# Forming the T4 sums of the feed-forward weights by accumulating DMA instead of on VectorE

## The chip, the cores and the metric

The kernel runs on one core of a Trainium2 chip. The metric is the device time of one execution in microseconds (us), less being better. Before the change it is 2789.99 us, the median of three runs (2787.24, 2789.99 and 2790.11).

## What is computed

One decoder layer for 512 tokens of width 2048 in float32: RMS norm, sliding-window attention beside RWKV-7 time mixing, gates, an output projection, then a SwiGLU feed-forward part with 5632 hidden channels and a final norm. The change is in the feed-forward part:

```python
h = rms_norm(x, norm_ffn[l])
x = x + (jax.nn.silu(h @ ffn_gate[l]) * (h @ ffn_up[l])) @ ffn_down[l]
return rms_norm(x, norm_final)
```

`ffn_gate` and `ffn_up` are 2048 x 5632, `ffn_down` is 5632 x 2048.

## The kernel before, in words

The front part (attention, time mixing, merge, output projection) takes the first half of the time and is not touched. The feed-forward part is a loop of 17 steps `j`: steps 0 to 10 (`j < CHUNKS`) do 512 gate and 512 up columns each, steps 11 to 16 the down projection. Each step is a two-by-two block product by the Winograd form of Strassen's method, with seven block products in place of eight. The weight is cut into four blocks B11, B12, B22 and B21, each in its own buffer (`wblock11` and so on; `tight` in the two last steps), and three sums replace blocks in place:

- T1 = B12 - B11 in B11's buffer (`t_one`, L1756)
- T3 = B22 - B12 in B12's buffer (`t_three`, L1762)
- T2 = T3 + B11 in B12's buffer, by two accumulating DMAs that GpSimd issues (L774), which add B11 from DRAM onto the buffer
- T4 = T2 - B21 in B21's buffer (`t_four`, L1768)

The products run in the order 1 (B11), 7 (T3), 5 (T1), 6 (T2), 2 (B21), 3 (B22), 4 (T4). A product has `depth(j)` items, 8 in steps 0 to 14 and 6 in steps 15 and 16. An item is one weight tile of 128 x 512. Float32 accuracy comes from splitting each tile: ScalarE copies it to float32r (`ring_high`, the high part, L804), VectorE subtracts that from the tile (`ring_low`, the low part, L1731), and TensorE does six matmuls with them (L2387, L2389, L2391, twice). The ring of high and low parts has four places, so ScalarE can begin an item only when TensorE is done with the item four before it.

Each engine runs its instructions in the order in which they are written; semaphores tie the engines together. VectorE does the low parts and, between them, the sums T1, T3 and T4 and the combinations of the results (`c_lower1`, `hidden2` and others; L1787, L1792, L1821, L1908). Semaphore `sums_ready` counts the sums, and `sum_of` says which count belongs to which. SyncE issues the weight loads (`load_block`, L651) for the next step as soon as a buffer is free, in two halves, in the order 11, 12, 22, 21. GpSimd issues T2's accumulates and, in the down steps, adds the results onto `sum_dram` (`add_sums`, L765). ScalarE's `sums_of_a` in product 4 of a down step first waits for the add of block 22's result to land. In the last step, blocks of that sum come back from DRAM (L716, L720) for the final norm, whose squares ScalarE takes between the high parts.

## Time and profile before

| | |
|---|---|
| median of three runs | 2789.99 us |
| the profiled execution | 2789.86 us |
| its span, first to last instruction | 2788.1 us |
| TensorE (PE) busy | 2734.5 us (98%) |
| VectorE (DVE) busy | 1795.1 us (64%) |
| ScalarE (ACT) busy | 1259.8 us (45%) |
| GpSimd (POOL) busy | 638.1 us (23%) |
| TensorE clock granted, mean | 0.996 of full |

All times in rows are us from the start of the span of that one execution. Busy shares are means over the whole span; what one product of one step does has to be read in its own stretch. An instruction's duration overlaps the next one's start by some 0.08 us on VectorE and ScalarE, so what an instruction adds to a full engine is the distance from start to start. "SPq" is SyncE's queue, where an entry is the issue of a DMA and not its transfer.

### The profile page before, as it was taken

Reading aid. Unit: us, or ns where it says so; the run is one execution under the profiler, and the core shown is the slowest. Engines: PE = TensorE matmul, PEld = TensorE weight load, DVE = VectorE, ACT = ScalarE, POOL = GpSimd, SP = SyncE. Lnnn points to the kernel's source line nnn. Section 1 sums busy time; section 2 is a strip of 40 time slices with the busy share of each in tenths; the row PEclk is TensorE's granted clock in tenths of the full one; section 3 lists DMA queues with packets and bytes.
Section 4 is the critical chain, followed back from the end, with each engine's and each line's share of the span. In section 5 each row is a group of like instructions: output and inputs, shape, how many; then the busy total and the mean of one; then the engine's idle time right before and its main releaser. Section 6 shows DMA issues by size and latency. Waiting matters only on the chain.

```text
span 2788.1 us, 37752 instructions
## 1 busy us (share of the span) xinstructions
PE 2734.5 (98%) x14290; PEld 2205.3 (79%) x14290; DVE 1795.1 (64%) x2893; ACT 1259.8 (45%) x2053; POOL 638.1 (23%) x485
## 2 busy tenths in 40 slices
PE   8999999999999999999999999999999999999997
PEld 7777777777777777888887888888888887888875
DVE  5657365364463564322258878888778888888885
ACT  5444343343343334223335555555555556555555
POOL 2323234233233343544430000000000000111121
PEclk9999999999999999999999999999999999999998
DMA  5222122222222223433445566545654577786873
GB/s 188 76 76 104 65 83 94 76 87 79 77 82 96 73 87 132 158 136 129 139 139 156 166 177 178 153 143 158 177 148 135 152 238 222 188 240 175 216 193 95
DMA packets 190611, 382.51 MB, mean 137 GB/s; under 512 B 9584, under 2 KB 84592, under 8 KB 175728
## 3 DMA queue, kind: packets, MB, share of 16 engines
q1 hardware_dynamic: 146608, 320.55, 33.3%
q0 software_dynamic: 29728, 45.09, 9.9%
q10 hardware_dynamic: 14112, 14.68, 1.5%
q8 instruction: 103, 1.69, 0.2%
q14 instruction: 60, 0.49, 0.1%
HBM read 328.91 MB, written 51.38 MB: 136 GB/s over the span
## 4 chain that ended last, share of the span: by engine, by line
PE 88%; DVE 4%; issue 3%; ACT 2%; DMA 1%; DVEq 1%; POOL 1%; SPq 0%; ACTq 0%; POOLq 0%
PE dense L1994 11%; PE dense L1996 11%; PE dense L1995 11%; PE work L2387 11%; PE work L2389 11%; PE work L2391 11%; PE dense L2387 3%; PE dense L2389 3%; PE dense L2391 3%; PE work L2162 1%; DVEq L1288 1%; PE work L2400 1%; PE work L2214 1%; PE work L1995 1%; PE work L1996 1%
## 5 line engine op out<-in xcount | busy, mean ns | idle before, releaser
L804 ACT ACTIVATE ring_hi<-wblock 128x512 fp32r<-128x512 f32 x840 | 528.6, 631 | 538.9 <-PE work L2391 361.4
L742 POOL TENSOR_TENSOR wlo<-raw,whi 128x512 fp32r<-128x512 f32 x400 | 541.5, 1384 | 896.3 <-ACT whi L804 896.3
L1731 DVE TENSOR_TENSOR ring_lo<-wblock,ring_hi 128x512 fp32r<-128x512 f32 x840 | 573.5, 688 | 175.7 <-ACT ring_hi L804 168.6
L2387 PE MATMUL work<-ring_hi,S_hi 128*128 128x512 f32 x1460 | 573.8, 393 | 15.5 <-DVE ring_lo L1731 15.4
L2391 PE MATMUL work<-ring_lo,S_hi 128*128 128x512 f32 x1460 | 569.5, 390 | 0.0
L2389 PE MATMUL work<-ring_hi,S_lo 128*128 128x512 f32 x1460 | 569.5, 390 | 0.0
L1994 PE MATMUL dense<-H_hi,whi 128*128 128x512 f32 x1208 | 504.9, 418 | 10.1 <-DVE H_lo L1316 8.6
L1996 PE MATMUL dense<-H_hi,wlo 128*128 128x512 f32 x1208 | 473.4, 392 | 0.0
L1995 PE MATMUL dense<-H_lo,whi 128*128 128x512 f32 x1208 | 473.1, 392 | 0.0
L804 ACT ACTIVATE whi<-raw 128x2048 fp32r<-128x2048 f32 (+1 forms) x109 | 198.1, 1820 | 473.0 <-PE dense L1996 388.4
L2387 PEld LDWEIGHTS work<-ring_hi,S_hi 128*128 128x128 f32 x1460 | 275.0, 188 | 81.1 <-DVE ring_lo L1731 21.7
L2391 PEld LDWEIGHTS work<-ring_lo,S_hi 128*128 128x128 f32 x1460 | 274.8, 188 | 57.7
L2389 PEld LDWEIGHTS work<-ring_hi,S_lo 128*128 128x128 f32 x1460 | 275.2, 188 | 55.4
L1994 PEld LDWEIGHTS dense<-H_hi,whi 128*128 128x128 f32 x1208 | 227.7, 188 | 81.7 <-issue 27.0
L1996 PEld LDWEIGHTS dense<-H_hi,wlo 128*128 128x128 f32 x1208 | 227.4, 188 | 50.0
L1995 PEld LDWEIGHTS dense<-H_lo,whi 128*128 128x128 f32 x1208 | 228.0, 189 | 45.0 <-issue 5.8
L774 POOL DMA_DIRECT2D wblock<-w_gu x22 | 28.4, 1290 | 797.9 <-DVE ring_lo L1731 797.9
L2387 PE MATMUL dense<-ring_hi,S_hi 128*128 128x512 f32 x388 | 153.0, 394 | 0.6 <-DVE ring_lo L1731 0.5
L2389 PE MATMUL dense<-ring_hi,S_lo 128*128 128x512 f32 x388 | 151.1, 389 | 0.0
L2391 PE MATMUL dense<-ring_lo,S_hi 128*128 128x512 f32 x388 | 151.0, 389 | 0.0
L1994 PE MATMUL dense<-M_hi,whi 128*128 128x512 f32 x256 | 101.1, 395 | 0.0
L1996 PE MATMUL dense<-M_hi,wlo 128*128 128x512 f32 x256 | 99.8, 390 | 0.0
(336 smaller groups left out, 3391.2 us busy)
## 6 DMA issues: line engine op xcount, KB each, us to landing
raw<-w_slots SPq DMA_DIRECT2D x101, 1024.0 KB, 4.8
wblock<-w_gu SPq DMA_DIRECT2D x88, 1024.0 KB, 9.6
wblock<-w_down SPq DMA_DIRECT2D x60, 512.0 KB, 7.0
wblock<-w_gu POOLq DMA_DIRECT2D x22, 1024.0 KB, 9.8
S_raw<-s_dram SPq DMA_DIRECT2D x14, 1024.0 KB, 8.0
tight<-w_down SPq DMA_DIRECT2D x20, 512.0 KB, 8.2
gates_dram<-gout ACTq DMA_DIRECT2D x32, 256.0 KB, 2.1
gin<-gates_dram SPq DMA_DIRECT2D x16, 512.0 KB, 3.6
```

The source lines that it names most:

```text
L742: done = nc.gpsimd.tensor_tensor(wlo[s][:, at], raw[s][:, at], whi[s][:, at].bitcast(f32), SUB)
L774: pool.dma_start(into, src, accum_op=ADD).then_inc(t2_added[h], 16)
L804: return A.activation(dst, src, ACT.Copy, scale=scale)
L1288: V.drain()
L1731: V.tensor_tensor(ring_lo[w % RING][:], of_tile(j, source[product], k), ring_hi[w % RING][:].bitcast(f32), SUB).then_inc(ring_lo_ready, 1)
L1994: PE.matmul(bank[:], whi[s][:, wk], hi[:, k, :], start=(k == first), stop=False)
L1995: PE.matmul(bank[:], whi[s][:, wk], lo[:, k, :], start=False, stop=False)
L1996: done = PE.matmul(bank[:], wlo[s][:, wk], hi[:, k, :], start=False, stop=(k == last))
L2162: done = PE.matmul(g_bank(2 * t + e)[:, half:half + 2 * P], src[heads[e], tok], zq[heads[e], t].rearrange("p a n -> p (a n)"), start=True, ...
L2387: PE.matmul(banks[a][:], S_hi[product][:, k, tok], high[:], start=(k == 0 and product not in (3, 2)), stop=False, skip_group_check=True)
L2389: PE.matmul(banks[a][:], S_lo[product][:, k, tok], high[:], start=False, stop=False, skip_group_check=True)
L2391: done = PE.matmul(banks[a][:], S_hi[product][:, k, tok], rest[:], start=False, stop=(k == depth(j) - 1), skip_group_check=True)
```

## The change

T4 is no longer computed on VectorE. ScalarE negates B21 in place, tile by tile, after product 2 has read it: tiles 0 to 3 among the last high parts of product 2, the rest among the first of product 3 (`negate`). When half the block is negated, and T2 stands, GpSimd issues a DMA from B12's buffer to B21's with an add, both in SBUF (`t4_added`). Product 4's high parts wait for that. B12's buffer is read later than before, so SyncE loads the next B12 after B22, and behind a wait for both accumulates. And VectorE's T1 sums, which need that block, begin at the third item of product 1 and are made up from item `n - 3` on. The other edits reuse semaphores. The core of the diff:

```diff
-SUM0 = [sum(3 * depth(i) for i in range(j)) for j in range(STEPS)]
+SUM0 = [sum(2 * depth(i) for i in range(j)) for j in range(STEPS)]
...
+        def half_of(j, h):
+
+            return slice(h * HK // 2 * P, min((h + 1) * HK // 2, depth(j)) * P)
...
-                sp.wait_ge(sums_ready, sum_of(j, 4, depth(j) - 1))
-                load_block(j + 1, 12)
                 sp.wait_ge(ring_lo_ready, after(j, 3))
                 load_block(j + 1, 22)
+                for h in range(2):
+                    sp.wait_ge(t4_added[h], 16 * (j + 1))
+                load_block(j + 1, 12)
                 load_s(j, 3)
                 sp.wait_ge(ring_lo_ready, after(j, 4))
                 load_block(j + 1, 21)
...
                         pool.dma_start(into, src, accum_op=ADD).then_inc(t2_added[h], 16)
+                for h in range(2):
+                    pool.wait_ge(t2_added[h], 16 * block_dmas(j, 11, h))
+                    pool.wait_ge(negated, SUM0[j] // 2 + min((h + 1) * HK // 2, depth(j)))
+                    pool.dma_start(blocks(j)[21][:, :, half_of(j, h)], blocks(j)[12][:, :, half_of(j, h)],
+                                   accum_op=ADD).then_inc(t4_added[h], 16)
...
+                elif product == 4:
+                    act.wait_ge(t4_added[2 * k // HK], 16 * (j + 1))
...
+            def negate(j, k):
+
+                act.wait_ge(ring_lo_ready, item_of(j, 2, k) + 1)
+                tile = blocks(j)[21][:, :, k * P:(k + 1) * P]
+                copy(tile, tile, -1.0).then_inc(negated, 1)
...
                     ring_high(j, 2, k)
+                    if k >= 4:
+                        negate(j, k - 4)
...
                     ring_high(j, 3, k)
+                    if k < 4:
+                        negate(j, depth(j) - 4 + k)
...
                         ring_low(j, 1, k)
-                    t_one(j, k)
-                    if k >= n - 2:
+                    if 2 <= k < n - 3:
+                        t_one(j, k - 2)
+                    if k == n - 3:
+                        t_one(j, n - 5)
+                        t_one(j, n - 4)
+                    if k == n - 2:
+                        t_one(j, n - 3)
+                        t_one(j, n - 2)
                         fence()
-                        t_three(j, k - n + 2)
+                        t_three(j, 0)
+                    if k == n - 1:
+                        t_one(j, n - 1)
+                        fence()
+                        t_three(j, 1)
...
-                    if k in (1, 2):
-                        fence()
-                        t_four(j, k - 1)
...
-                    if k + 2 < n:
-                        fence()
-                        t_four(j, k + 2)
```

VectorE in product 1 of a gate/up step, before. A row is one instruction in program order with the tile that it writes and those that it reads; `ring_lo` rows are low parts, `wblock11<-wblock12` is T1, `u3buf` is `c_lower1`.

```order
L1731 TENSOR_TENSOR ring_lo0_196<-wblock11_188,ring_hi0_192 128x512
L1756 TENSOR_TENSOR wblock11_188<-wblock12_189,wblock11_188 128x4x128
L1731 TENSOR_TENSOR ring_lo1_197<-wblock11_188,ring_hi1_193 128x512
L1756 TENSOR_TENSOR wblock11_188<-wblock12_189,wblock11_188 128x4x128
L1731 TENSOR_TENSOR ring_lo2_198<-wblock11_188,ring_hi2_194 128x512
L1756 TENSOR_TENSOR wblock11_188<-wblock12_189,wblock11_188 128x4x128
L1731 TENSOR_TENSOR ring_lo3_199<-wblock11_188,ring_hi3_195 128x512
L1756 TENSOR_TENSOR wblock11_188<-wblock12_189,wblock11_188 128x4x128
L1787 TENSOR_TENSOR u3buf_201<-u3buf_201,work4 128x512
```

The same place after the change, from the first low part of product 1 to T3's first sum (`wblock12<-wblock22`).

```order
L1754 TENSOR_TENSOR ring_lo0_196<-wblock11_188,ring_hi0_192 128x512
L1754 TENSOR_TENSOR ring_lo1_197<-wblock11_188,ring_hi1_193 128x512
L1754 TENSOR_TENSOR ring_lo2_198<-wblock11_188,ring_hi2_194 128x512
L1779 TENSOR_TENSOR wblock11_188<-wblock12_189,wblock11_188 128x4x128
L1754 TENSOR_TENSOR ring_lo3_199<-wblock11_188,ring_hi3_195 128x512
L1779 TENSOR_TENSOR wblock11_188<-wblock12_189,wblock11_188 128x4x128
L1804 TENSOR_TENSOR u3buf_201<-u3buf_201,work4 128x512
L1754 TENSOR_TENSOR ring_lo0_196<-wblock11_188,ring_hi0_192 128x512
L1779 TENSOR_TENSOR wblock11_188<-wblock12_189,wblock11_188 128x4x128
L1804 TENSOR_TENSOR u3buf_201<-u3buf_201,work5 128x512
L1754 TENSOR_TENSOR ring_lo1_197<-wblock11_188,ring_hi1_193 128x512
L1779 TENSOR_TENSOR wblock11_188<-wblock12_189,wblock11_188 128x4x128 x2
```

The first two low parts have no T1 behind them any more; two of the later ones have two.

SyncE's queue, the loads for the next step in a gate/up step, before:

```order
L651 DMA wblock11_188<-w_gu 128x4x512 [waits ring_lo_ready]
L651 DMA wblock11_188<-w_gu 128x4x512
L651 DMA wblock12_189<-w_gu 128x4x512 [waits sums_ready]
L651 DMA wblock12_189<-w_gu 128x4x512
L651 DMA wblock22_190<-w_gu 128x4x512 [waits ring_lo_ready]
L651 DMA wblock22_190<-w_gu 128x4x512
L651 DMA wblock21_191<-w_gu 128x4x512 [waits ring_lo_ready]
L651 DMA wblock21_191<-w_gu 128x4x512
```

and after:

```order
L656 DMA wblock11_188<-w_gu 128x4x512 [waits ring_lo_ready]
L656 DMA wblock11_188<-w_gu 128x4x512
L656 DMA wblock22_190<-w_gu 128x4x512 [waits ring_lo_ready]
L656 DMA wblock22_190<-w_gu 128x4x512
L656 DMA wblock12_189<-w_gu 128x4x512 [waits t4_added1,t4_added0]
L656 DMA wblock12_189<-w_gu 128x4x512
L656 DMA wblock21_191<-w_gu 128x4x512 [waits ring_lo_ready]
L656 DMA wblock21_191<-w_gu 128x4x512
```

B12's load has gone behind B22's and waits for the accumulates; B21's load is queued behind it.

GpSimd's queue in the first down step after the change; before, the two rows of L784 were not there, and the first `sum_dram` row followed T2's directly.

```order
L780 DMA wblock12_189<-w_down 128x4x256 [waits ring_lo_ready]
L780 DMA wblock12_189<-w_down 128x4x256
L784 DMA wblock21_191<-wblock12_189 128x4x512 [waits negated,t2_added0]
L784 DMA wblock21_191<-wblock12_189 128x4x512 [waits negated,t2_added1]
L771 DMA sum_dram<-c22buf_202 128x2x512 [waits c_ready,xt_stored]
```

The add of block 22's result onto `sum_dram` is now issued behind both accumulates of T4.

## Rows read from the trace of the kernel before

**Rows 1.** Busy time by stretch: a gate/up step's length, a down step's

```profile
1759.20:1835.70 76.50, 76.48 (x346) 63.18 (x345) 62.16 (x97) 39.19 (x65) 2.56 (x2) 1.00 0.57 162
2447.70:2524.20 76.50, 75.86 (x335) 62.28 (x334) 67.41 (x95) 44.58 (x65) 10.04 (x8) 1.00 0.81 220
```

**Rows 2.** What TensorE waited for, 1455 to 2740: total, times, longest

```profile
PE work L2387 <- DVE ring_lo L1731: 15.4, 10, 6.2
```

**Rows 3.** Chain of waits, the last loads of final sums: start, length

```profile
2709.95 13.79 DMA fin<-sum_dram
```

**Rows 4.** Timeline of VectorE, step 4, products 1 and 7

```profile
1780.58 0.69 DVE L1731 TENSOR_TENSOR ring_lo<-wblock,ring_hi 128x512 fp32r<-128x512 f32 x1 [0.17 <-ACT ring_hi L804]
...
1783.17 0.68 DVE L1756 TENSOR_TENSOR wblock<-wblock,wblock 128x512 f32<-128x512 f32 x1
1783.78 0.69 DVE L1731 TENSOR_TENSOR ring_lo<-wblock,ring_hi 128x512 fp32r<-128x512 f32 x1
...
1792.70 0.69 DVE L1731 TENSOR_TENSOR ring_lo<-wblock,ring_hi 128x512 fp32r<-128x512 f32 x1
```

**Rows 5.** Timeline of TensorE, step 4: product 7's first and fourth item

```profile
1789.18 0.39 PE L2387 MATMUL dense<-ring_hi,S_hi 128*128 128x512 f32 x1
...
1793.44 0.50 PE L2387 MATMUL dense<-ring_hi,S_hi 128*128 128x512 f32 x1
```

**Rows 6.** Timeline of ScalarE, step 4: product 2's last item, products 3 and 4

```profile
1828.72 0.63 ACT L804 ACTIVATE ring_hi<-wblock 128x512 fp32r<-128x512 f32 x1 [0.73 <-PE work L2391]
...
1834.70 0.64 ACT L1116 ACTIVATE work<-work,rstd 128x512 f32<-128x512 f32 x1
...
1840.96 0.63 ACT L804 ACTIVATE ring_hi<-wblock 128x512 fp32r<-128x512 f32 x1 [0.73 <-PE work L2391]
...
1846.40 0.63 ACT L804 ACTIVATE ring_hi<-wblock 128x512 fp32r<-128x512 f32 x1 [0.73 <-PE work L2391]
```

**Rows 7.** Timeline of VectorE, step 12, product 7's first low part

```profile
2417.38 0.68 DVE L1731 TENSOR_TENSOR ring_lo<-wblock,ring_hi 128x512 fp32r<-128x512 f32 x1
```

**Rows 8.** Timeline of TensorE, step 12, product 7's first item

```profile
2418.21 0.47 PE L2387 MATMUL dense<-ring_hi,S_hi 128*128 128x512 f32 x1
```

**Rows 9.** Timeline of VectorE, step 11, product 1's second low part

```profile
2326.14 0.68 DVE L1731 TENSOR_TENSOR ring_lo<-wblock,ring_hi 128x512 fp32r<-128x512 f32 x1
```

**Rows 10.** Timeline of GpSimd, step 4: T2's two accumulates

```profile
1793.68 1.28 POOL L774 DMA_DIRECT2D wblock<-w_gu  x1 [72.58 <-DVE ring_lo L1731]
1798.08 1.28 POOL L774 DMA_DIRECT2D wblock<-w_gu  x1 [3.12 <-DVE ring_lo L1731]
```

**Rows 11.** Line L774 in 1780 to 1800, those two: issue to landing

```profile
DMA to landing us min/median/max: 9.5/9.8/10.1
```

**Rows 12.** DMA queues in 1793 to 1809: packets, MB, share of 16 engines

```profile
q0 software_dynamic: 1056, 2.10, 77.0%
```

**Rows 13.** DMA queues in 1760 to 1786, plain loads: the same columns

```profile
q1 hardware_dynamic: 3440, 6.82, 79.2%
```

**Rows 14.** Timeline of SyncE, the six loads of B12, B22, B21

```profile
1761.95 12.78 SPq L651 DMA_DIRECT2D wblock<-w_gu  x6
```

**Rows 15.** Line L651 in 1763.1 to 1763.5, the third of the six: landing

```profile
DMA to landing us min/median/max: 10.7/10.7/10.7
```

**Rows 16.** Timeline of VectorE, step 5, product 1's third T1 sum

```profile
1855.84 0.68 DVE L1756 TENSOR_TENSOR wblock<-wblock,wblock 128x512 f32<-128x512 f32 x1
```

**Rows 17.** Timeline of ScalarE, step 15: second of product 3, product 4's first, `sums_of_a`

```profile
2677.17 0.63 ACT L804 ACTIVATE ring_hi<-tight 128x512 fp32r<-128x512 f32 x1 [0.73 <-PE dense L2391]
...
2684.99 0.63 ACT L804 ACTIVATE ring_hi<-tight 128x512 fp32r<-128x512 f32 x1 [0.75 <-PE work L2391]
...
2689.65 0.58 ACT L804 ACTIVATE c22buf<-dense 128x512 f32<-128x512 f32 x1
```

**Rows 18.** Timeline of GpSimd, step 15: block 22's sum

```profile
2680.07 1.20 POOL L765 DMA_DIRECT2D sum_dram<-c22buf  x1 [25.53 <-DVE c22buf L1908]
```

**Rows 19.** What TensorE waited for, 1459.5 to 1468.6, in step 0

```profile
PE work L2387 <- DVE ring_lo L1731: 4.5, 1, 4.5
```

More of the change, by code:

```diff
@@ L145, in sum_of @@
     n = depth(j)
-    first = {5: k + 1 + max(k - n + 2, 0), 7: (n + 2 * k if k < 2 else n + 1 + k), 4: 2 * n + 1 + k}[product]
+    first = {5: k + 1 + max(k - n + 2, 0), 7: (n + 2 * k if k < 2 else n + 1 + k)}[product]
     return SUM0[j] + first
@@ L440, in build_layer @@
         sums_ready, t2_added = sem("sums_ready"), [sem(f"t2_added{h}") for h in range(2)]
+        negated, t4_added = sem("negated"), [sem(f"t4_added{h}") for h in range(2)]
         ring_hi_ready, ring_lo_ready, item_done = (
@@ L449, in build_layer @@
         added = {b: sem(f"added{b}") for b in block_at}
-        fin1_loaded, fin0_loaded, gin_before = sem("fin1_loaded"), gin_loaded, 8 * KD
+        fin1_loaded, fin0_loaded, gin_before, xin_before = xin_loaded[0], gin_loaded, 8 * KD, 8 * KD
         fin_ready, fin_squared, fin_turned, resid_copied = (
@@ L454, in build_layer @@
         tail_inverse, tail_spread, scale_copied = sem("tail_inverse"), sem("tail_spread"), sem("scale_copied")
-        pool_out, out_ready, out_stored = sem("pool_out"), sem("out_ready"), sem("out_stored")
+        pool_out, out_ready, out_stored = sem("pool_out"), sem("out_ready"), xin_loaded[1]
         heads = [slice(e * HD, e * HD + HD) for e in range(2)]
@@ L730, in _ @@
                                  ).then_inc(out_stored, 16)
-            sp.wait_ge(out_stored, 2 * 16 * len(OUT_PARTS))
+            sp.wait_ge(out_stored, xin_before + 2 * 16 * len(OUT_PARTS))
         @block.gpsimd
@@ L1763, in t_three @@
                                 ).then_inc(sums_ready, 1)
-            def t_four(j, k):
-                block_wait(dve, j, 21, k)
-                V.tensor_tensor(of_tile(j, 21, k), of_tile(j, 12, k), of_tile(j, 21, k), SUB
-                                ).then_inc(sums_ready, 1)
             def s_late_low(place_of, product):
@@ L1863, in _ @@
                         dve.wait_ge(item_done, after(j, 7))
-                        dve.wait_ge(fin1_loaded, 64)
+                        dve.wait_ge(fin1_loaded, xin_before + 64)
                         add_to(fin1[21][a], bank_of(j, 7)[a][:])
```

## The prediction, made before the changed kernel ran

> **What bounds the kernel now.** I read busy time by stretch first. In a gate/up step TensorE is busy 76.48 us of 76.50, in a down step 75.86 [rows 1]. VectorE, from which the change takes work, is busy 62 to 67 us there: it has spare time, but TensorE has none to give back. Next, what TensorE waited for: between 1455 and 2740 it stood 15.4 us behind low parts, ten times, 6.2 us of it once in the last step [rows 2]. That is all that a faster VectorE could win, and the 6.2 us belong to the final sums coming back by DMA [rows 3]. So the question is not what the change frees, but whether it moves something into TensorE's way. For that I read the timelines of one steady step.
>
> VectorE is not evenly loaded. Step 4's fifth low part of product 1 still waits for its high part (0.17 us idle, at 1780.58); from there to the low part at 1792.70, the fourth item of product 7, no idle is marked [rows 4]. That low part ends at 1792.70 + 0.69 = 1793.39, and TensorE starts on it at 1793.44 [rows 5]: 0.05 us apart. Product 7's first item to its fourth took 4.26 us, where three items at TensorE's pace are 4.08 (1.36 us each: four high parts of product 4 from 1840.96 to 1846.40 [rows 6]). So VectorE has just used up its whole lead there. Products 1 and 7 are the one place in a step where VectorE is on the path, and T4 is not computed there.
>
> **T4 off VectorE.** Its 132 sums go (8 in a deep step), each 0.60 us from start to start by the like sum T1, 1783.17 to 1783.78 [rows 4]. They stood in products 2 and 3, which in steady steps hold TensorE up nowhere. Gain: 0 there. Where VectorE is behind in products 2 and 3 (step 15, by its S splits) I give some tenths, inside the term for that step.
>
> **T1 later.** This is the costly part. Before, each low part of product 1 had a T1 behind it, in time in which VectorE would have waited for ScalarE anyway. Now the first two have none, and these two sums come after the fifth item, in the stretch without idle. Up to the fifth low part nothing changes in time, since ScalarE sets it. From there to product 7's fourth item VectorE has the same work as before and two T1 sums more: 2 x 0.60 = 1.20 us. T3 comes late by the same, and so do product 7's high parts, which wait for it, but each is still ready before its low part. With 0.05 us of margin, TensorE stands the 1.20 us, in two to four pieces over product 7.
>
> Steps 1 to 10 repeat this pattern: 10 x 1.20 = 12.0 us. In step 12 the tightest item is product 7's first: low part done at 2417.38 + 0.68 = 2418.06, TensorE at 2418.21, 0.15 apart [rows 7, 8], so 0.10 more is left than the 0.05: 1.10 us, and steps 12 to 15 alike: 4.4 us. Step 11 starts with VectorE in arrears: its second low part, at 2326.14, comes without idle before it [rows 9], and the two sums that are missing there first let it catch up. Between 0 and 1.20 I take 0.4. In step 0 the first low parts are made ahead of the loop; the two sums leave an early wait of TensorE shorter and make a later one longer, 0. In step 16 the 1.10 us come ahead of the wait for the final sums, which ends by DMA and not by TensorE's time: 0 (at most 1.1).
>
> **The accumulate.** The trace has no transfer within SBUF that adds, but T2's add from DRAM with the same shape: 9.5 and 10.1 us from issue to landing, issued 4.4 us apart [rows 10, 11], the two taking 77% of 16 us, or 12.3 us of all engines, for 2.10 MB [rows 12]. The first half of T4 is negated after product 2's last high part: 1828.72 + 0.54 + 0.63 = 1829.9, issued some 0.3 us later (as long as T2's issue at 1793.68 comes after the low part's end at 1793.39), landing at 1830.2 + 9.5 = 1839.7. Product 4's first high part starts at 1840.96 [rows 6]: 1.3 us to spare. A high part's successor on ScalarE starts 0.54 us after it, as L1116 at 1834.70 does (its high part is five paces before 1840.96, at 1834.16). The second half's last negation takes that place and ends at 1835.3; issued at 1835.6, landed at 1845.7, wanted at 1846.40: 0.7 us to spare, and behind that stands the ring's lead. So 0 in deep steps. That lead is at most 2.7 us: a high part starts when TensorE ends the item four before, so three items (4.08 us) ahead, less some 1.4 us for the high and the low part. So 0 in deep steps. Bounds: plain loads take 79.2% of 26 us for 6.82 MB, 3.0 us a MB [rows 13] against 5.9 for the adds; at that pace T4 lands up to 6 us sooner and still gains 0. At half T2's pace the pair needs 24.6 us and lands some 12 us later, about 9 us beyond the lead in each of the 17 steps. I take T2's own pace, the nearest row.
>
> The Trainium skill ("DMA: Bandwidth & Descriptors", section on the anatomy of one DMA on the SWDGE path) gives 2.0 us plus bytes over 436 GB/s for a DMA from GpSimd, an estimate of 4.4 us for 1 MB. The trace disagrees for adds: 9.5 us [rows 11]. By the page the allowances for T4 below would be 0 and the sum some 3 us less.
>
> **The negations.** 132 on ScalarE, about 0.54 us more each beside a high part in a pace of 1.36 us: 0.54 + 0.54 = 1.08, it fits. Where L1116 stands too, 1.62 once or twice, inside the lead. 0.
>
> **Loads.** B22 goes out when product 3's low parts are done, about 1841.1 (one pace before 1840.96, plus a high and a low part), B12 at T4's landing, 1845.7. Before, the third load of a row lands at 1763.16 + 10.7 = 1773.9, 11.9 us after the first was issued at 1761.95 [rows 14, 15]. So B12's first half lands at 1841.1 + 11.9 = 1853.0, and with up to 1.3 us lost to T4's tail at 1854.4. The first T1 now stands where the third stood, 1855.84 [rows 16]: 1.4 us to spare. Then 0, but thin: VectorE would wait in front of all low parts, and every us late is a us of each step. In down steps SyncE's nine to eleven issues and the three result adds run at the same time (DMA share 0.81 [rows 1]), and there it is a matter of nothing to 2 us a step.
>
> The Trainium skill (same page, "Issuing engines are not separate DMA queues") says that transfers of all issuers share the 16 engines. If T4's adds therefore slow B22's and B12's loads by more than the 1.3 us allowed, it is the first rival below.
>
> **Shallow step 15.** Here product 3 has six items, and T4's first half is ready only after its second high part: 2677.17 + 1.2 = 2678.4, issued 2678.7, landed 2688.2, wanted at 2684.99 [rows 17]. ScalarE is 3.2 us late, TensorE behind its lead some 0.7. Then block 22's add, issued at 2680.07 before [rows 18], goes out behind T4's second half, near 2683, and through the same queue: it lands near 2694.5, where `sums_of_a` (2689.65 [rows 17]) wants it, 5 us late, some 2 of it beyond the lead. This also moves the chain of final sums that ends the wait in step 16. I take 3.0 us together, bounds 0 and 7.
>
> **Sum.** 12.0 + 0.4 + 4.4 + 3.0 = 19.8 us. 2789.86 + 19.8 = 2809.7; the profiled execution is 0.13 us under the median shown. Forecast: 2810 us, slower by 0.7%. Its own range is 2803 to 2818 (step 11 and 15 at their ends, step 16's 1.1, a us of loads in some down steps).
>
> **Rivals.**
>
> 1. The transfers are late, beside the late sums. Place: B12's first half lands after the first T1's place. It decides from 1.4 us more than reckoned, and each further us costs 16. At 2 us late per step: 2810 + 32 = 2842. For it: the engines are full in both rows that matter, and B22's and B12's loads had them to themselves before. Against: T4 is nearly through when B22's data starts. With T4 itself at half pace it would be 2940 and more.
>
> 2. The same time, 2790. The two late sums are absorbed, since the arrears of VectorE are made up in a way that I do not see, or the stall shortens a later one. Against: 0.05 us between low part and matmul [rows 4, 5], and no later stall in steady steps to shorten [rows 1].
>
> 3. Faster: VectorE without T4 carries a longer lead into the other stalls [rows 2] in steps 10 to 15, and takes them away. Place: product 4 and the next product 1; it decides if the lead at the start of product 1 is VectorE's and not the ring's. Price: of 15.4 us, 6.2 are the final sums' and 4.5 lie in step 0 [rows 19], so about 4.7 us: 2785. Against: the ring has four places, and the high part waits for TensorE, not VectorE, on nearly every item of product 4 [rows 6].
>
> **Chances.** Forecast 0.63, rival 1 0.22, rival 2 0.09, rival 3 0.06. A measurement of this kernel can tell about 0.2%, 5.6 us, from no change. So slower by more 0.85, within 0.09, faster 0.06. The range: 2797 to 2845, which leaves out rivals 2 and 3 and the far end of rival 1.
>
> **What would show it.** Steps 1 to 10 last 1.2 us longer each, with TensorE waiting for low parts in items one to four of product 7 and not in products 2, 3 and 4. No low part of product 4 follows a ScalarE wait for DMA, except in step 15. The accumulate lands in 9 to 10.5 us. VectorE's busy time falls by about 132 x 0.69 = 91 us, ScalarE's rises by some 80. Wrong if TensorE's waits stand in product 1 (B12 late) or 4 (T4 late), or if a steady step keeps its length.

## The result: 46 us slower, and the profile after

The changed kernel takes 2836.3 us (median of 4 runs, 2835.87 to 2836.71) against 2789.98 (4 runs, 2787.24 to 2790.11), measured beside it: a ratio of 1.017, 95% interval 1.0157 to 1.0183. The forecast was 2810, so the sign was right and the loss was more than twice what I reckoned. Its profiled execution spans 2834.3 us, 46.2 more than before's.

The head of the page of the changed kernel, two lines of its queues and two of its DMA issues (KB each, median us from issue to landing):

```profile
PE 2750.9 (97%) x14290; PEld 2206.6 (78%) x14290; DVE 1715.6 (61%) x2761; ACT 1324.9 (47%) x2185; POOL 681.6 (24%) x519
...
q1 hardware_dynamic: 146608, 320.55, 32.2%
q0 software_dynamic: 47680, 79.70, 16.8%
...
wblock<-wblock POOLq DMA_DIRECT2D x30, 1024.0 KB, 8.4
...
wblock<-w_gu POOLq DMA_DIRECT2D x22, 1024.0 KB, 9.9
```

VectorE is busy 79.5 us less than before, ScalarE 65.1 us more (forecast: about 91 less and 80 more), and T4's accumulates land in 8.4 us in the median, a little sooner than T2's 9.9. None of these three explains 46 us. Where the time went is read from the length of each step, from its first matmul to the next step's first (step 16: to within 0.1 us of the next matmul behind it), in the timeline of TensorE. This table has them, in us, for all kernels of the study; "late sums" and the other names are the experiments of the next section.

| kernel | steps 1 to 9, mean | 10 | 11 | 12 | 13 | 14 | 15 | 16 |
|---|---|---|---|---|---|---|---|---|
| before | 78.26 | 79.59 | 79.94 | 77.24 | 76.32 | 76.31 | 59.85 | 73.50 |
| changed | 79.52 | 83.25 | 80.45 | 85.76 | 84.13 | 84.14 | 70.13 | 72.63 |
| late sums alone | 79.48 | 80.83 | 80.42 | 78.45 | 77.50 | 77.53 | 60.89 | 74.23 |
| gate/up alone | 79.50 | 83.37 | 79.98 | 77.26 | 76.32 | 76.35 | 59.89 | 73.33 |
| B12 first | 79.50 | 83.52 | 80.40 | 79.05 | 78.17 | 77.74 | 63.96 | 81.12 |
| sum 22 first | 79.51 | 83.25 | 80.39 | 90.06 | 77.49 | 82.91 | 63.61 | 75.17 |
| old T1 order | 78.91 | 84.55 | 79.21 | 88.01 | 84.89 | 84.98 | 71.21 | 75.64 |
| late loads, no T4 transfer | 79.46 | 80.79 | 80.36 | 78.41 | 77.49 | 77.57 | 60.51 | 71.63 |
| B12 and sum 22 first | 79.51 | 83.47 | 80.39 | 82.44 | 77.66 | 79.49 | 62.31 | 80.52 |
| B12 first, S later | 79.50 | 80.79 | 80.37 | 78.46 | 78.01 | 77.52 | 62.31 | 78.81 |
| repaired, old T1 order | 78.26 | 79.88 | 79.95 | 77.25 | 81.75 | 76.68 | 62.60 | 78.49 |
| and shallow steps as before | 78.26 | 79.59 | 79.97 | 77.25 | 82.53 | 76.67 | 61.05 | 72.57 |
| and S later in step 10 only | 78.26 | 79.55 | 79.98 | 77.92 | 79.05 | 76.99 | 64.12 | 72.50 |

Steps 1 to 9 are 1.26 us longer each, as forecast. Step 10 is 3.7 longer, and steps 12 to 15 are 34.4 us longer together (8.5, 7.8, 7.8, 10.3), where the forecast had 7.4 (4.4 for the late sums and 3.0 for the shallow step). Step 16 is even 0.9 shorter. Steps 1 to 16 together lose 49 us; the span loses 46.2, since step 0 is 0.9 us shorter and starts 1.9 sooner. Its start lies between 1455.6 and 1458.6 us in the thirteen kernels, which all have the same front part, so a us or two of a difference between two spans can come from there.

What TensorE waited for in the changed kernel, 2345 to the end (total, times, longest), the answer to [rows 2]; in before the same stretch has 10.3 us behind low parts:

```profile
PE work L2408 <- DVE ring_lo L1754: 21.9, 16, 3.6
PE dense L2408 <- DVE ring_lo L1754: 10.6, 7, 4.1
```

The low parts are late because VectorE is held in front of them. What it waited for in that stretch (these waits for loads exist only in the changed kernel):

```profile
DVE wblock L1779 <- DMA wblock<-w_down: 18.3, 3, 6.7
DVE tight L1779 <- DMA tight<-w_down: 10.3, 2, 5.5
```

Line 1779 is T1, which reads B12. So in each of steps 12 to 16 the first T1 waits for that load, 28.6 us in all. Here it is in step 12, first the timeline of VectorE, then that of TensorE, which uses the low part of 2427.09:

```profile
2419.57 0.69 DVE L1754 TENSOR_TENSOR ring_lo<-wblock,ring_hi 128x512 fp32r<-128x512 f32 x1 [0.67 <-ACT ring_hi L815]
2426.48 0.69 DVE L1779 TENSOR_TENSOR wblock<-wblock,wblock 128x512 f32<-128x512 f32 x1 [6.22 <-DMA wblock<-w_down]
2427.09 0.68 DVE L1754 TENSOR_TENSOR ring_lo<-wblock,ring_hi 128x512 fp32r<-128x512 f32 x1
```

```profile
2427.83 0.50 PE L2408 MATMUL work<-ring_hi,S_hi 128*128 128x512 f32 x1 [3.58 <-DVE ring_lo L1754]
```

Of 6.22 us, 2.6 are TensorE's lead and 3.6 are lost. VectorE, with no lead left, then costs 0.83 at product 1's last item, where the late sums alone cost 0.36. Why is the load late? GpSimd's timeline around it, then what the queues did in the same 16 us (packets, MB, share of 16 engines):

```profile
2394.78 1.29 POOL L784 DMA_DIRECT2D wblock<-wblock  x1 [31.52 <-ACT wblock L815]
2400.22 1.29 POOL L784 DMA_DIRECT2D wblock<-wblock  x1 [4.14 <-ACT wblock L815]
2400.97 1.76 POOL L771 DMA_DIRECT2D sum_dram<-c22buf  x1
```

```profile
q0 software_dynamic: 1328, 2.62, 98.7%
q1 hardware_dynamic: 297, 0.30, 5.6%
```

T4's two halves and block 22's result sum fill the 16 DMA engines from 2396 to 2412. SyncE has issued B22 from 2405.33 on, but nearly none of its data has moved by 2412. Its issues slow down with it: the pieces of B22 take up to 2.1 us each to issue, so B12's, free to go since T4 landed at 2400.22 + 8.72 = 2408.94, go out from 2412.30 to 2416.33. The first two, which T1 waits for, are issued at 2412.3 and 2413.6:

```profile
L656 SPq DMA_DIRECT2D wblock<-w_down x2: 1216/1621/2026, 2412.3 to 2413.6; - x2
...
  DVE wblock L1779: 6.2, 1
...
DMA to landing us min/median/max: 12.0/12.5/12.9
```

2413.56 + 12.89 = 2426.45, and T1 starts at 2426.48.

The same two stretches as [rows 1] of a gate/up and a down step (start:end, length, PE, PEld, DVE, ACT and POOL busy, clock, DMA share, GB/s), and a piece of the second at half clock:

```profile
1759.50:1836.00 76.50, 75.89 (x341) 61.95 (x340) 57.51 (x89) 42.02 (x70) 4.72 (x4) 1.00 0.66 182
2506.00:2590.10 84.10, 78.68 (x337) 63.92 (x336) 61.47 (x87) 47.75 (x72) 12.62 (x10) 0.98 0.81 203
...
2429.00:2432.40 3.40, 3.40 (x9) 2.21 (x8) 3.31 (x7) 0.63 (x1) 0.79 (x1) 0.50 1.12 369
```

The third line is a price on top. From 1.1 us after the wait that ends at 2427.83 the granted clock is 0.50 for 3.4 us (1.2 GHz in place of 2.4), and a matmul takes 0.43 us from start to start (2430.83 to 2431.26) in place of 0.23. From step 10 to 16 the changed kernel has five such stretches, 20.5 us, at five of its six waits of 2.7 us or more (three of them begin while TensorE still waits, so a part of them costs nothing), where before has one of 6.8 us: 13.7 us more at half speed, up to 6.8 us of the 46.

### The profile page after: what moved, and what is told of

Read it like the earlier page. It is cut to its first block, busy times and chain, and to the rows that moved or that the text cites. A ratio compares the mean times of both kernels' runs of the same rounds, so it can differ in the third digit from the quotient of the medians.

```text
span 2834.3 us, 37704 instructions
## 1 busy us (share of the span) xinstructions
PE 2750.9 (97%) x14290; PEld 2206.6 (78%) x14290; DVE 1715.6 (61%) x2761; ACT 1324.9 (47%) x2185; POOL 681.6 (24%) x519
## 3 DMA queue, kind: packets, MB, share of 16 engines
q0 software_dynamic: 47680, 79.70, 16.8%
## 4 chain that ended last, share of the span: by engine, by line
PE 79%; DVE 9%; DMA 5%; ACT 3%; issue 2%; DVEq 2%; SPq 1%; POOL 0%; ACTq 0%; POOLq 0%
PE dense L2015 11%; PE dense L2017 11%; PE dense L2016 11%; PE work L2408 9%; PE work L2410 9%; PE work L2412 9%; DVE ring_lo L1754 2%; PE dense L2408 2%; PE dense L2412 2%; PE dense L2410 2%; DVE wblock L1779 2%; DVEq L1311 2%; DVE wblock L1785 2%; DMA wblock<-w_down 1%; DMA wblock<-wblock 1%
## 5 line engine op out<-in xcount | busy, mean ns | idle before, releaser
L2015 PE MATMUL dense<-H_hi,whi 128*128 128x512 f32 x1208 | 504.7, 418 | 10.1 <-DVE H_lo L1339 8.6
L2408 PE MATMUL dense<-ring_hi,S_hi 128*128 128x512 f32 x388 | 156.2, 403 | 14.2 <-DVE ring_lo L1754 13.9
L784 POOL DMA_DIRECT2D wblock<-wblock x30 | 38.6, 1286 | 524.3 <-ACT wblock L815 524.3
L2408 PEld LDWEIGHTS dense<-ring_hi,S_hi 128*128 128x128 f32 x388 | 73.6, 190 | 39.7 <-DVE ring_lo L1754 23.1
```

The lines of the kernel that those rows point to most:

```text
L2015: PE.matmul(bank[:], whi[s][:, wk], hi[:, k, :], start=(k == first), stop=False)
L2408: PE.matmul(banks[a][:], S_hi[product][:, k, tok], high[:], start=(k == 0 and product not in (3, 2)), stop=False, skip_group_check=True)
```

## The experiments

The intervals are 95%. The kernel before was run again beside each group of experiments, and it differs by up to 2 us between groups, so a difference of that size between two medians of different groups says little; before measured 2787.92 us (7 runs, 2785.57 to 2790.16) beside the first four, 2787.81 (7 runs, 2786.83 to 2791.19) beside the next four, and 2789.07 and 2789.42 (10 runs each) beside the last three.

**Late sums alone.** The kernel before with T1's new order and nothing else.

```diff
-                    t_one(j, k)
+                    if 2 <= k < n - 3:
+                        t_one(j, k - 2)
...
```

> The kernel before with one part of the change: T1's sums stand where the change puts them (first one behind the third low part of product 1, two each behind the sixth and seventh). T4 stays on VectorE, the loads keep their order. If the late sums are a cause by themselves, as forecast (1.2 us in steps 1 to 10, some 1.1 in 12 to 15, 0.4 in 11, less up to 1 in step 0): 2805 us, 2802 to 2808, with waits for low parts in product 7 only. If the 1.2 us that the changed kernel shows in its steps 1 to 9 come from T4's transfers or the negations instead: 2790.

Measured 2804.89 us (4 runs, 2802.87 to 2806.78), ratio 1.0061 (1.0044 to 1.0078). As expected. By steps: 12.3 us in steps 1 to 10 (forecast 12.0), 0.5 in step 11 (0.4), 4.65 in steps 12 to 15 (4.4).

**Gate/up alone.** T4 by DMA, B12's later load and the late sums in steps 0 to 10 only; the down steps as before.

```diff
-                for h in range(2):
+                for h in range(2 if j < CHUNKS else 0):
                     pool.wait_ge(t2_added[h], 16 * block_dmas(j, 11, h))
...
```

> The changed kernel with the change in the eleven gate/up steps only; steps 11 to 16 have T4 on VectorE, T1 behind every low part and the old order of loads, except the loads for step 11, which step 10 issues in the new order. If the excess over the forecast lies in the down steps: 2790 + 11.5 for steps 1 to 10, less 0.9 in step 0, and 0 to 3 for step 10's waits in product 4: 2800 to 2804. If the transfers of the gate/up steps carried part of the loss into the down steps: 2810 or more.

Measured 2802.08 (2800.3 to 2802.45), ratio 1.0049 (1.0033 to 1.0066). As expected: the excess belongs to the down steps, but for step 10, which keeps its 83.37.

**B12 first.** The changed kernel with the loads of B12 and B22 in the old order, B12's still behind T4's landing.

```diff
+                for h in range(2):
+                    sp.wait_ge(t4_added[h], 16 * (j + 1))
+                load_block(j + 1, 12)
                 sp.wait_ge(ring_lo_ready, after(j, 3))
                 load_block(j + 1, 22)
-                for h in range(2):
-                    sp.wait_ge(t4_added[h], 16 * (j + 1))
-                load_block(j + 1, 12)
```

> The changed kernel with B12's load ahead of B22's in SyncE's queue, still behind both waits for T4's accumulates. Theory Q (queueing): in the down steps B12 is late because its pieces are issued and moved behind the five pieces of B22; then they land some 6 to 8 us earlier, before the first T1 sum wants them, TensorE's waits in product 1 of steps 12 to 16 and the half clock after them go, and the time is 2808 to 2814. Theory T (traffic): B12 is late because T4's accumulates land late and take the engines; then the order matters little: 2825 to 2833. Gate/up steps keep their 79.5 us under both.

Measured 2817.67 (2816.96 to 2819.86), ratio 1.0107 (1.009 to 1.0123). It lies between the two expectations, over the 2814 of the queueing theory and well under the 2825 of the traffic theory. It wins 18.6 us back, 16.6 if each kernel is taken against its own before, and steps 12 to 15, 324.2 us in the changed kernel, take 298.9, 4.5 over the late sums alone. So T4's landing itself comes early enough for B12; what is lost is lost between it and B12's data. Step 10 stays at 83.5: its one wait of 1.85 us brings 3.4 us at half clock with it, so it isn't the length of a wait alone that decides. Step 16 grows to 81.1: part of what is won comes back there as waits of 5.6 us at most, with 6.8 and twice 3.4 us at half clock.

**Sum 22 first.** The changed kernel with block 22's result sum issued between T4's halves, since ScalarE waited 11.3 us in all for it (its line is below).

```diff
+                    if h == 0 and CHUNKS <= j < LAST:
...
+                        add_sums(j, 22, c22buf)
```

> The changed kernel with the add of block 22's result onto DRAM issued between T4's two accumulates instead of behind both (down steps only). ScalarE's waits for that add, 11.3 us in three pieces (steps 12, 14 and 15), should go nearly. If they are worth their share of TensorE's waits in product 4 (1.8, 1.1 and 3.3 us, with the half clock in step 15): 2828 to 2832. If T4's second half, now some 3 us later, delays product 4 and B12's load by as much: no change or slower, 2836 to 2845.

Measured 2829.34 (2828.02 to 2830.82), ratio 1.0148 (1.0131 to 1.0165): 7.0 us better than the change (4.9 against each one's own before), within the first of the two expectations. ScalarE's wait for the sum is down to 0.7 us, and steps 13 and 15 fall by 6.6 and 6.5. But steps 12 and 14 are 90.1 and 82.9 us: the file of transfers (all that is queued for the 16 engines, in order) has another order and the same length, so T4's second half is late in product 4 instead (TensorE waits 2.5 and 1.5 us there in step 12), and in steps 12, 14 and 16 B12 still is in product 1.

**Late loads, no T4 transfer.** Late sums alone, and from the loads for step 12 on B22's load first and B12's behind product 4's fourth low part. Now place and traffic are apart.

```diff
-                sp.wait_ge(sums_ready, sum_of(j, 4, depth(j) - 1))
-                load_block(j + 1, 12)
+                if j < CHUNKS:
+                    sp.wait_ge(sums_ready, sum_of(j, 4, depth(j) - 1))
+                    load_block(j + 1, 12)
                 sp.wait_ge(ring_lo_ready, after(j, 3))
                 load_block(j + 1, 22)
+                if j >= CHUNKS:
+                    sp.wait_ge(ring_lo_ready, item_of(j, 4, 3))
+                    load_block(j + 1, 12)
```

> The kernel before with T1's late order (as in the experiment on the late sums alone, 2804.9 us) and one more edit: from step 11 on, block 22's load goes first and block 12's goes out behind it and behind product 4's fourth low part, which is the moment at which the changed kernel issues it. T4 stays on VectorE, so no T4 transfer shares the queues. Theory 'place' (block 12's late place behind block 22's five pieces is enough): VectorE again waits some 4.5 to 6 us for block 12 at product 1's third low part in steps 12 to 16, TensorE 2 to 3.6 us and some tenths after it, so each of these steps is 4 to 6.5 us longer than in the experiment on the late sums: 2825 to 2838. Theory 'traffic' (T4's two transfers, and block 22's result sum that queues behind them, are what push block 12 out): block 12 lands some 3 us and more sooner, and the time is 2805 to 2813. Values between say that both have a share, and the share is (time - 2805) / (2836 - 2805).

Measured 2804.18 (2802.1 to 2804.9), ratio 1.0054 (1.0037 to 1.0071): the late sums' time, share 0 for the place. The queues of this kernel in 2396 to 2412, then the load of B12's second piece, issued at 2409.5 behind all of B22:

```profile
q1 hardware_dynamic: 2449, 1.92, 37.8%
q0 software_dynamic: 272, 0.52, 23.1%
```

```profile
L651 SPq DMA_DIRECT2D wblock<-w_down x1: 739/739/739, 2409.5 to 2409.5; - x1
...
DMA to landing us min/median/max: 7.4/7.4/7.4
```

It lands at 2416.9, 9.6 us sooner than in the changed kernel, and T1 wants it at 2419.81. The difference between the two q0 lines is T4: 98.7% - 23.1% of 16 us, 12.1 us of all engines. B12 behind B22 is harmless with the engines free, and behind T4 and the sum it costs 6 to 6.7 us a step (steps 12 to 15 of the changed kernel against B12 first); B12 first behind T4 costs 0.2 to 0.7 in the deep ones. It takes both together: a place behind B22, and T4's transfers in front. (This kernel also has no negations on ScalarE and T4's sums on VectorE; the rows above show the load itself on time.)

**Old T1 order.** The changed kernel with T1's sums back at their places.

```diff
-                    if 2 <= k < n - 3:
-                        t_one(j, k - 2)
...
+                    t_one(j, k)
```

> The changed kernel with one thing undone: T1's sums stand where they did before, the first behind product 1's first low part. The loads and T4's transfers stay as changed. Theory 'coupled' (the late order was needed because block 12 now lands late): in a gate/up step block 12's first half lands at 1856.9 and the first T1 would be wanted near 1853.1, so VectorE waits some 3.8 us in front of the low parts, of which about 2 us are idle time that it has in product 1's first items anyway; TensorE loses 1.5 to 2.5 us a step in place of the 1.2 of the late order, and in the five down steps the wait for block 12 grows by up to two items (2.7 us) less the 1.1 of the late sums: 2836 + 10 x (0.3 to 1.3) + 5 x 1.6 = 2847 to 2857. Theory 'needless' (the late order only costs, and block 12 is early enough in gate/up steps): steps 1 to 10 get their 1.2 us back and the whole lands at 2822 to 2830.

Measured 2839.98 (2837.46 to 2842.09), ratio 1.0182 (1.0165 to 1.0199). Neither expectation. Steps 1 to 9 take 78.91, 0.6 us less than with the late order, though B12 lands as late: there the late order costs more than the wait that it avoids. In the down steps TensorE now waits at product 1's second item:

```profile
2425.17 0.79 PE L2398 MATMUL work<-ring_hi,S_hi 128*128 128x512 f32 x1 [6.41 <-DVE ring_lo L1754]
```

The five waits are 5.4 to 6.4 us, where the late order had 2.7 to 4.1. With the half clock that comes with them (10.2 us from 2421, which begins inside the first wait, and 6.8 in each of the four others) these steps take 404.7 us against 396.8. The late order is worth something there, 7.9 us in five steps, and by the experiment on the repaired kernel below only because the load is late.

**B12 and sum 22 first.** Both repairs.

> The changed kernel with both repairs tried singly so far: block 12's load ahead of block 22's (alone 2817.7 us) and the result sum of block 22 between T4's two halves (alone 2829.3, 7 us better than the change). If the two gains belong to different waits (block 12 for VectorE's T1; the result sum for ScalarE's reuse of its buffer in steps 12, 14 and 15), they add up: 2817.7 less 2 to 5 = 2812 to 2816. If they are the same wait seen twice (the whole file of transfers moved up), the second adds nothing, or T4's second half, now behind the result sum, costs in product 4: 2816 to 2822.

Measured 2823.2 (2822.2 to 2824.1), ratio 1.0123 (1.0106 to 1.014): 5.5 us worse than B12 first alone, just outside the second expectation, on its side. Steps 12 and 14 take 82.4 and 79.5; TensorE waits 0.92 and 1.92 us in product 4 of step 12 for T4's second half, now behind the sum. The gains don't add.

**B12 first, S later.** B12 first, and the load of product 2's S rows moved behind both block loads. It goes out in steps 10, 12 and 14 only, beside T4's transfers.

```diff
-                load_s(j, 2)
...
                 load_block(j + 1, 22)
+                load_s(j, 2)
                 load_s(j, 3)
```

> The changed kernel with block 12's load first (alone 2817.7 us) and the load of product 2's S rows (steps 10, 12 and 14 only) moved from product 2's end, beside T4's transfers, behind both block loads. In step 10 of the changed kernel this S load is issued at 2313.68, and T4's second half, issued at 2315.46, lands 13.9 us later where 8.6 is usual; TensorE then waits 0.84 + 1.92 us in product 4. If the S load is what holds the transfer up, step 10 falls from 83.5 to 80.7 - 81.3 us, steps 12 and 14 by some tenths to 1 us, and the whole to 2812.5 to 2815.5. If T4's second half is late by its own wait and not by the S load, step 10 stays at 83 to 84 us and the whole at 2817 to 2820.

Measured 2812.85 (2811.72 to 2816.17), ratio 1.0091 (1.0074 to 1.0108). As expected: step 10 falls from 83.5 to 80.8, the value of the late sums alone. The transfer that made it long (the same happens in steps 12 and 14, 12.4 and 12.5 us to landing in the changed kernel, 8.7 and 8.8 here), T4's second half at 2315.5 in the changed kernel, and the same one here:

```profile
L784 POOL DMA_DIRECT2D wblock<-wblock x1: 1287/1287/1287, 2315.5 to 2315.5; - x1
...
DMA to landing us min/median/max: 13.9/13.9/13.9
```

```profile
L784 POOL DMA_DIRECT2D wblock<-wblock x1: 1284/1284/1284, 2315.0 to 2315.0; - x1
...
DMA to landing us min/median/max: 9.7/9.7/9.7
```

Steps 1 to 14 are those of the late sums within 0.5 us. What is left lies in steps 15 and 16, 1.4 and 4.6 us of the 6.3 by which the two profiled spans differ.

**Repaired, old T1 order.** B12 first, S later, and T1 at its old places.

> The changed kernel with block 12's load first, the S load behind both block loads (these two alone: 2812.9 us), and T1's sums back in their old order. Theory 'load order was the only reason for the late order': with block 12 first, its first half lands at 1852.6 in a gate/up step and at 2413.2 in a down step, where the old order wants the first T1 near 1855.3 and 2414.6: 2.7 and 1.3 us to spare. Then the late sums' cost goes (12.3 us in steps 1 to 10, 0.5 in step 11, about 3.5 in steps 12 to 14 and up to 1 in step 15), steps 1 to 9 fall to 78.25 - 78.35, and the time is 2794 to 2799. Theory 'margin too thin': VectorE, at T1's old place, waits for block 12 in the down steps, or for block 22 at T3, which now also comes 1.2 us sooner; then steps 12 to 14 stay at 78 us and more, and the time is 2800 to 2808.

Measured 2803.82 (5 runs, 2802.61 to 2808.18), ratio 1.0057 (1.0043 to 1.0071). Neither expectation as a whole. The time is in the second's range, the reason is not the second's: neither B12 nor B22 is late in steps 12 to 14. The cost of the late sums is gone: steps 1 to 12 are before's within 0.3 us, so with B12 first nothing asks for the late order there. But step 13 takes 81.75, with a wait of TensorE of 3.5 us in product 5.

**And shallow steps as before.** T4 of steps 15 and 16 on VectorE again; 120 of the 132 sums stay with the DMA (the expectation miscounts them as 118).

> The same kernel with one more edit: in steps 15 and 16, with six items a product, T4 is computed on VectorE as in the kernel before; T4 by DMA stays in steps 0 to 14. Theory 'shallow steps hold the rest': step 15 falls back to 59.9 and step 16 to 73 - 74 us, so the time is that of the kernel before within what can be told, 2787 to 2793, with 118 of 132 sums off VectorE and nothing won by it. Rival: T4 by DMA costs elsewhere too, or the freed VectorE wins something once nothing is late: then the time is over 2794, or under 2785.

Measured 2797.83 (6 runs, 2795.39 to 2802.64), ratio 1.0035 (1.0023 to 1.0047): over the first expectation, so its rival is right that T4 costs elsewhere too. Steps 15 and 16 lose 1.6 and 5.9 us of what they had; step 13 stays at 82.5. ScalarE's timeline there:

```profile
2511.73 1.91 ACT L818 ACTIVATE S_hi<-S_raw 128x2048 fp32r<-128x2048 f32 x1 [5.98 <-DMA S_raw<-s_dram]
```

**And S later in step 10 only.**

```diff
+                if j != CHUNKS - 1:
+                    load_s(j, 2)
...
+                if j == CHUNKS - 1:
+                    load_s(j, 2)
```

> The repaired kernel with T4 by DMA in steps 0 to 14 (2797.8 us), with the load of product 2's S rows moved behind the block loads in step 10 only; in steps 12 and 14 it goes out at product 2's end again. In that kernel ScalarE waits 8.4 us in all, up to 6.0, for S rows, and step 13 takes 82.5 us where 76.3 is usual, with TensorE's wait of 4.5 us in product 5: the S load of step 12, now late, should be the reason. If it is, step 13 falls to 76.3 - 76.7, steps 12 and 14 gain at most 0.6 us, and the time is 2789 to 2793, that of the kernel before within what can be told. If the wait in step 13 has another source (block 11's load, the result sums), step 13 stays over 80 us and the time at 2795 to 2800.

Measured 2796.18 (6 runs, 2794.5 to 2800.45), ratio 1.0027 (1.0015 to 1.0039). A miss of the first expectation; the time is in the second's range, but step 13 isn't over 80. It falls by 3.5 us to 79.05, so the late S load was part of it, but step 12 gains 0.7 and step 15 3.1 again. The 0.7 is T4 once more: with the S load beside it its second half lands after 11.9 us in place of 8.6, and TensorE waits 1.31 us in product 4 of step 12 in place of 0.64. With T4 in the queues the down steps 12 to 16 take 370.1 us with the one order and 370.6 with the other, 363.2 before. I can move the 7 us from step to step, not away; which transfer costs the rest of them stays open. In steps 1 to 11 of these two kernels, where before has 0.54 to 0.73 of the engines busy, T4 by DMA is free, and VectorE's spared time has won nothing there, 78.26 us a step as before. None of the kernels beats the one before.

## Why the prediction was right in sign and wrong in size

**T4 off VectorE, 0: held.** 79.5 us less work, and no step shorter for it.

**T1 later, 12.0 + 0.4 + 4.4: held.** In step 4 of the changed kernel TensorE waits at product 7's first item and at its fourth, and nowhere else in the step.

```profile
1790.94 0.50 PE L2408 MATMUL dense<-ring_hi,S_hi 128*128 128x512 f32 x1 [0.35 <-DVE ring_lo L1754]
...
1795.88 0.50 PE L2408 MATMUL dense<-ring_hi,S_hi 128*128 128x512 f32 x1 [0.21 <-DVE ring_lo L1754]
```

The marked waits do not sum to 1.2; the rest lies in slower starts around them (1793.57 to 1794.02 in the same product). The experiment on the late sums measured 17.0 us for them as a whole, against 16.8.

**The accumulate, 0 in deep steps: held, except in steps 10, 12 and 14.** In step 4 it lands in 7.8 and 8.1 us, sooner than T2's 9.5 and 10.1 [rows 11], and no high part of product 4 waits. Its engine time is T2's: 12.2 us for 2.10 MB against 12.3 [rows 12]. In steps 10, 12 and 14 an S load (1 MB, in step 14 0.75) is issued 1.8 to 2.1 us before T4's second half, which I had not looked for. The half then lands after 13.9, 12.4 and 12.5 us, and product 4 waits for it, against my sign that this happens in step 15 alone: 2.4 us of step 10, and 1.2 and 1.1 us more than before of TensorE's waits in product 4 of steps 12 and 14, shared with the sum of block 22 behind it.

**Loads: this is the step that failed.** I wrote "there it is a matter of nothing to 2 us a step" and took 0. For gate/up steps I worked out the landing of B12's first half (1854.4; the trace has 1846.51 + 10.43 = 1856.9, 2.5 us later and still without a loss, since the first T1 comes at about 1858). For the down steps I did not do the sum. It was in the rows: [rows 1] has the engines busy 0.81 of 76.5 us, 62 us, and T4 adds 12.3 [rows 12], 0.97, an estimate. I charged T4's 12 us of engine time to T4's own landing and only 1.3 us of it to the loads behind it. Block 22's sum, which I made late for step 15, stands in the same file in every down step: 3.7 us (23.1% of 16) between T4 and B22. Measured from the table: 324.2 us in steps 12 to 15 against 294.4 with the late sums alone, 29.8 us, of which B12's place behind T4's file is 25.2 (what B12 first wins back). Rival 1 had the mechanism, the wait in front of T1 and nearly the total (2842), but spread at 2 us over all 16 steps; it was 6.6 to 9.2 us in each of steps 12 to 15 (changed against late sums alone), and none in the others but step 10, whose 2.4 us are the S load's.

**Half clock: not in the sum.** Up to 6.8 of these 46 us. Five of six waits of TensorE of 2.7 us or more brought 3.4 or 6.8 us at 1.2 GHz with them, and the forecast priced waits at their length.

**Shallow step 15, 3.0: close, where it can be seen alone.** With B12 first, step 15 is 3.1 us over the late sums. In the changed kernel its timeline on ScalarE has both waits that I named, product 4's first high part for T4 and `sums_of_a` for the sum of block 22:

```profile
2729.35 2.20 ACT L815 ACTIVATE ring_hi<-tight 128x512 fp32r<-128x512 f32 x4 [3.87 <-DMA tight<-tight]
2737.99 0.60 ACT L815 ACTIVATE c22buf<-dense 128x512 f32<-128x512 f32 x1 [6.44 <-DMA sum_dram<-c22buf]
```

3.87 us for the one (3.2 forecast) and 6.44 for the other (5). TensorE lost 0.67 us behind the first (0.7 forecast) and 3.34 behind the second, where I had some 2. The like wait for block 22's sum is there in steps 12 and 14 too, where I looked for none, and with it the one for T4's second half; in 2345 to the end:

```profile
ACT c22buf L815 <- DMA sum_dram<-c22buf: 11.3, 3, 6.4
...
ACT ring_hi L815 <- DMA wblock<-wblock: 4.1, 2, 2.2
```

**Step 16, 0: the number held by luck.** It is 0.9 us shorter: TensorE's wait of 6.2 us for final sums [rows 2, 3] is gone, since the work in front of them is now later than they are, and with it its 6.8 us at half clock. Waits of 2.8, 0.9 and 0.95 us in product 1 and a new one of 1.8 us for the residual stand in its place, 7.2 us in all against 7.0. Where the earlier steps are repaired, the step takes 78.5 to 81.1 us with T4 by DMA, and 72.6 with T4 of the two shallow steps on VectorE: the transfers do cost there, 5.9 us in the one pair of kernels that differ in this alone.

## What to carry to other kernels

A transfer that is moved onto the DMA engines has two prices: when it lands, and the engine time that it takes from whatever is issued behind it. The second is checked by adding its engine time to the busy share of each kind of stage (here 0.81 + 12.1 / 76.5 = 0.97 in the down steps, an estimate), and then by following the whole file there, every transfer in order, not only in the stage with the most room. The share alone is a warning and no verdict: by whole steps before has 0.86, 0.72 and 0.80 in steps 12 to 14, and the kernel with B12 first and S later has 0.95, 0.89 and 0.90 there and is as fast as the late sums alone within 0.5 us. What cost was which load stood behind the adds. A stage that is worked out for its easy case says nothing of its crowded one, and a wait with which TensorE's clock falls costs more than its length.

## What the runs showed of the hardware

- An accumulating transfer within SBUF (1 MB, 128x512 tiles) took 7.7 to 9.2 us to land in gate/up steps 0 to 9 and 7.9 to 8.8 in down steps 11 and 13. Behind a load of S rows issued 1.8 to 2.1 us before it on the other queue it took 13.9 (step 10), 12.4 and 12.5 (steps 12 and 14); with that load moved away, 9.7, 8.7 and 8.8. The like add from DRAM took 9.5 and 10.1.
- An issue on SyncE's queue took 0.37 to 0.67 us where the engines were free (late loads, no T4 transfer: B22's five pieces 2405.03 to 2407.09) and 0.4 to 2.1 us where a backlog stood (changed kernel: 2405.33 to 2410.19 for the same five). Later loads of the same files took up to 4.1 us to issue in the changed kernel, and 5.7 without T4 and 4.3 before, so long issues are not T4's alone. Under a backlog the next load is late twice, by its issue and by its transfer: B12's second piece was free to go at 2408.94, was issued at 2413.56 and took 12.9 us, against 7.4 with the engines free.
- Two queues' lines for 2405 to 2427 in the changed kernel add up to 110% of 16 engines, so a share near or over 1 here means full, not a quantity.

```profile
q0 software_dynamic: 1073, 2.07, 56.0%
q1 hardware_dynamic: 4442, 3.89, 53.5%
```
